# Sample attention first, its output weights split beside it; prompt attention and the sample's top-k moved into the output-projection stage

## The chip, the core and the metric

The kernel runs on one core of one Trainium2 chip. The metric is the device time of one execution in microseconds. On a core, TensorE (PE) multiplies, VectorE (DVE) and ScalarE (ACT) work elementwise, GpSimd (POOL) issues the indirect transfers and SyncE (SP) most of the others. Each engine takes its own instructions strictly in the order of the program and stops at a semaphore wait until it is met; whatever stands behind the wait on that engine waits too.

## What is computed

One encoder layer over two token sets that share all weights: a prompt of 512 tokens and a sample of 1024, width 1024. Cut to what matters:

```python
q, k, v, ca, cg = split(h @ w_in)                  # h: normed, modulated x
attn_out = neighbourhood_attention(q, k, v, rpb)   # 8 heads of 64, 8x16 window on a 64-wide grid
conv_out = conformer_conv(ca, cg, ...)
mix = concat([attn_out, conv_out], -1) @ w_out
x = x + gate1 * mix
h2 = rms_norm(x, norm2_g) * (1 + scale2) + shift2
aff = softmax(h2 @ w_router)                       # 16 experts
g, idx = top_k(aff.T, cap)                         # cap = 128 for the sample, 64 for the prompt
ye = swiglu(h2[idx], w_gate[e], w_up[e], w_down[e]) * g
x = x + gate2 * scatter_add(ye, idx)
```

The prompt and the sample are two sets: each expert takes the best 64 tokens of the prompt and the best 128 of the sample.

## The kernel before

Four functions follow each other, each with a block in which every engine has its own program; a block ends when all engines have ended theirs.

- `front`: per 128-token tile the norm of x and its transposes, the conditioning (`ada_w`, 12 loads of 2 MB), then the input projection as products of f32r high and low parts, with the convolution's taps on VectorE beside them. At its start VectorE first waits for all constants (`consts`, L691), and TensorE does so before the first transpose; the identity matrix is the first of them, issued on ScalarE's queue. The load of x tile t waits until tile t-3 has been normed.
- `attend`: 48 pairs of units in the order head pair, then block: 4 blocks of the prompt (256 keys) and 8 of the sample (384 keys) per head pair. A pair is: scores for two heads (TensorE), bias and maximum (L907, VectorE), exponential (L941, ScalarE), reciprocal and scaling (L914, L917), transposes (L862), their copy (L949), the product with v (L877), copy out (L926). The queues issue q and k of head pair 0, two heads' biases, 64 loads of v on SyncE and 32 on ScalarE, then the rest.
- `mix`: loads `w_out` (4 MB) and splits it into high and low parts (L1081, L1118), then 12 tiles in order, prompt first: split of the input (L1076 to L1113), 48 matmuls (L1041), gate and residual add (L1131, L1134), sum of squares (L1088), root, reciprocal, scaling (L1143), 8 transposes (L1051), modulation on ScalarE (L1096), the router's matmul (L1059), softmax, transpose (L1066), copy into `affT` (L1166). Tile t's matmuls, tile t-1's norm and tile t-2's softmax go side by side.
- `experts`: starts the weight loads; VectorE does 16 rounds of top-8 over `affT`, 48 rows x 1024 (rows 0 to 15 are the prompt's experts, 32 to 47 the sample's), each a MAX8 (L1506), FIND_INDEX8 (L1508) and MATCH_REPLACE8 (L1510). Then the lists are turned, POOL gathers the rows of expert 0 (L1358, L1360), and 16 experts follow. Each expert is bound by TensorE.

The text on record counts tiles of `mix` as steps 0 to 11, with two steps of run-out behind them.

Of the kernel before, what the change touches and what calls it, by code (L numbers as in the profile page):

```python
# [32 lines left out]
F32 = mybir.dt.float32  # L33
# [6 lines left out]
P = 128  # L40
# [41 lines left out]
def program(nc, A, outs):  # L82
# [29 lines left out]
    with g:  # L112
# [12 lines left out]
        affT = sb(g, "affT", [48, SAMPLE])  # L125
        o_ctx = ExitStack()
        with o_ctx:
            attn = sb(o_ctx, "attn", [P, 4, TOKENS])
            attend(nc, A, sem, sb, ps, qk_d, v_d, ident, attn)
            mix(nc, A, sem, sb, ps, rows_of, x_d, y_d, ada_d, conv_d, xhat_d, ident, eps_col, modv, a2, affT, attn)  # L130
        experts(nc, A, sem, sb, ps, y_d, ada_d, xhat_d, ident, modv, a2, affT)
# [31 lines left out]
def front(nc, A, sem, sb, ps, ada_d, rows_of, x_d, qk_d, conv_d, v_d,  # L163
# [49 lines left out]
    with ExitStack() as c:  # L213
# [49 lines left out]
        CONSTS = 16 * (5 + CG)  # L263
# [47 lines left out]
        with nc.Block() as block:  # L311
            @block.sync
            def _(sp):
# [18 lines left out]
                load_x(0)  # L332
                load_x(1)
# [67 lines left out]
            def _(pe):  # L401
# [40 lines left out]
                def side(job):  # L442
# [9 lines left out]
                    else:  # L452
                        pe.wait_ge(ada_row, MODS)
# [21 lines left out]
                pe.wait_ge(consts, CONSTS)  # L475
# [67 lines left out]
            def _(act):  # L543
                act.dma_start(ident[:, :], A["ident"]).then_inc(consts, 16)
# [6 lines left out]
                act.wait_ge(c_loaded, 32)  # L551
# [115 lines left out]
            def _(dve):  # L667
# [22 lines left out]

                dve.wait_ge(consts, CONSTS)  # L691
                dve.tensor_scalar(qkg[:, 0:1], qkg[:, 0:1], DH ** -0.5, None, ALU.mult).then_inc(qkg_ready, 1)
                for t in range(TILES):
# [6 lines left out]
                    if t == 5:  # L700
                        ada_rows(0)
# [76 lines left out]
def attend(nc, A, sem, sb, ps, qk_d, v_d, ident, attn):  # L778

    NB = len(BLOCKS)
    UNITS = HEADS * NB
    PAIRS = UNITS // 2
    PR = 6
    qk_loaded = [sem(f"qk_loaded{i}") for i in range(4)]
    v_loaded = [sem(f"v_loaded{i}") for i in range(len(V_ROWS))]
    bias_loaded = [sem(f"bias_loaded{i}") for i in range(4)]
    s_done, s_biased, p_ready, p_scaled = (
        sem("s_done"), sem("s_biased"), sem("p_ready"), sem("p_scaled"))  # L790
    pT_done, pT_out, o_done, r_ready, o_out = sem("pT_done"), sem("pT_out"), sem("o_done"), sem("r_ready"), sem("o_out")
# [858 lines left out]
```

## Time and profile before

| | us |
|---|---|
| median of 3 runs (range) | 3412.8 (3410.8 to 3413.2) |
| profiled execution: its own time | 3411.5 |
| its span | 3409.3 |
| mean granted TensorE clock | 0.965 |
| TensorE busy | 3169.9 (93%) |
| VectorE busy | 2298.9 (67%) |
| ScalarE busy | 1911.0 (56%) |

The page divides the span into 40 slices of 85 us. TensorE is at nine tenths or more in every slice behind the eleventh, in the sixth to eighth, which hold `attend`, at seven, and in the eleventh, the top-k, nearly idle. A stage's worth is therefore read from its own stretch and not from the busy shares of the span.

### The profile page before, as it was taken

What the parts mean: (1) busy time and instruction counts of PE and PEld (TensorE: products, weight loads), DVE (VectorE), ACT (ScalarE), POOL (GpSimd) and SP (SyncE); (2) the same over time, 40 slices, a digit from 0 to 9 for tenths busy, and PEclk for the clock granted to TensorE, in tenths of its full rate; (3) what the DMA queues carried; (4) which work ended last, traced back from release to release, by engine and by line L of the source; (5) the groups of instructions that cost most, each with busy time, mean ns of one, the idle gap of its engine ahead of it and who ended that gap; (6) DMA issues with size and microseconds to landing.
All of it is one profiled execution on the core that took longest, in us unless ns stands there. A gap on an engine that the chain in (4) does not pass through costs nothing.

```text
span 3409.3 us, 50511 instructions
## 1 busy us (share of the span) xinstructions
PE 3169.9 (93%) x18950; PEld 2832.9 (83%) x18950; DVE 2298.9 (67%) x3457; ACT 1911.0 (56%) x3096; POOL 150.8 (4%) x209
## 2 busy tenths in 40 slices
PE   5999877798099999999999999999999999999997
PEld 3777654587089999999999999999999999999997
DVE  4678815633757776767677776767677676767675
ACT  5143435655056666666666665666666666666654
POOL 0000000000000100101010010101010010101000
PEclk8999988999589999999999999999999999999999
DMA  8321137232345766657575765757576665757572
GB/s 308 130 62 53 47 100 248 104 131 93 146 178 218 264 231 241 241 201 275 193 288 218 251 237 226 254 206 277 194 273 226 241 250 221 263 187 278 210 253 87
DMA packets 136261, 690.67 MB, mean 203 GB/s; under 512 B 12032, under 2 KB 39824, under 8 KB 112528
## 3 DMA queue, kind: packets, MB, share of 16 engines
q1 hardware_dynamic: 125824, 659.68, 51.9%
q0 software_dynamic: 7168, 25.17, 3.2%
q10 hardware_dynamic: 3088, 3.10, 0.3%
q8 instruction: 152, 2.49, 0.3%
q14 instruction: 29, 0.24, 0.0%
HBM read 650.14 MB, written 37.77 MB: 202 GB/s over the span
## 4 chain that ended last, share of the span: by engine, by line
PE 72%; DVE 2%; DMA 0%; POOL 0%; ACT 0%; issue 0%; POOLq 0%; DVEq 0%
PE psG L1318 32%; PE psG L1320 15%; PE psY L1334 5%; PE psY L1337 5%; PE psY L1335 5%; PE psY L1336 5%; PE psY L1338 5%; DVE idxu L1508 1%; DVE affT L1510 1%; DVE vals L1506 1%; PE psG L1285 0%; PE psG L1286 0%; DMA xg_s<-xhat_d,inow 0%; ACT xst L1417 0%; DVE xe L1529 0%
## 5 line engine op out<-in xcount | busy, mean ns | idle before, releaser
L1318 PE MATMUL psG<-xe,w_gu_hi_part 128*128 128x384 f32 x5632 | 1630.8, 360 | 4.2 <-DVE xe L1529 4.2
L1320 PE MATMUL psG<-xe,w_gu_lo_part 128*128 128x192 f32 x5632 | 1411.3, 251 | 0.0
L1320 PEld LDWEIGHTS psG<-xe,w_gu_lo_part 128*128 128x128 f32 x5632 | 1076.9, 191 | 7.9
L1318 PEld LDWEIGHTS psG<-xe,w_gu_hi_part 128*128 128x128 f32 x5632 | 1058.9, 188 | 12.6 <-DVE xe L1529 4.6
L1519 DVE TENSOR_TENSOR w_gu_lo_part<-raw_gu,w_gu_hi_part 128x1024 fp32r<-128x1024 f32 x704 | 858.8, 1222 | 117.8 <-ACT w_gu_hi_part L1428 117.8
L1428 ACT ACTIVATE w_gu_hi_part<-raw_gu 128x1024 fp32r<-128x1024 f32 x704 | 741.2, 1055 | 13.1 <-DMA raw_gu<-in_w_gu 13.1
L1553 DVE TENSOR_TENSOR gu<-psG,low 128x384 f32<-128x384 f32 x352 | 195.7, 556 | 569.3 <-ACT low L1458 569.3
L1524 DVE TENSOR_TENSOR w_dn_lo_part<-raw_dn,w_dn_hi_part 128x1024 fp32r<-128x1024 f32 x352 | 431.0, 1224 | 0.5 <-ACT w_dn_hi_part L1439 0.5
L1458 ACT ACTIVATE low<-psG 128x384 f32<-128x384 f32 x352 | 172.0, 489 | 417.0 <-PE psG L1320 417.0
L1439 ACT ACTIVATE w_dn_hi_part<-raw_dn 128x1024 fp32r<-128x1024 f32 x352 | 367.7, 1045 | 0.8 <-PE psY L1338 0.8
L1417 ACT ACTIVATE xst<-psG,modv,a 128x128 f32<-128x128 f32 (+1 forms) x256 | 95.7, 425 | 392.2 <-PE psG L1320 325.4
L1334 PE MATMUL psY<-w_dn_hi_part,hs 128*128 128x512 f32 x704 | 282.6, 401 | 0.0
L1337 PE MATMUL psY<-w_dn_hi_part,hs 128*128 128x512 f32 x704 | 277.7, 394 | 0.0
L1335 PE MATMUL psY<-w_dn_lo_part,hs 128*128 128x512 f32 x704 | 276.5, 393 | 0.0
L1336 PE MATMUL psY<-w_dn_hi_part,hs 128*128 128x512 f32 x704 | 276.1, 392 | 0.0
L1338 PE MATMUL psY<-w_dn_lo_part,hs 128*128 128x512 f32 x704 | 274.2, 389 | 0.0
L663 DVE SCALAR_TENSOR_TENSOR shared<-shared,convp 128x1566 f32<-128x1566 f32 x120 | 221.9, 1849 | 3.5
L438 PE MATMUL psZ<-h_hi,w_hi 128*128 128x512 f32 x480 | 202.9, 423 | 8.0 <-DVE h_lo L716 8.0
L1473 ACT ACTIVATE hs<-hid 128x192 fp32r<-128x192 f32 x352 | 128.4, 365 | 144.5 <-DVE hid L1560 144.4
L439 PE MATMUL psZ<-h_lo,w_hi 128*128 128x512 f32 x480 | 189.5, 395 | 0.0
L440 PE MATMUL psZ<-h_hi,w_lo 128*128 128x512 f32 x480 | 189.4, 395 | 0.0
L1337 PEld LDWEIGHTS psY<-w_dn_hi_part,hs 128*128 128x128 f32 x704 | 132.0, 187 | 30.6
(161 smaller groups left out, 3185.3 us busy)
## 6 DMA issues: line engine op xcount, KB each, us to landing
raw_gu<-in_w_gu SPq DMA_DIRECT2D x176, 2048.0 KB, 7.9
raw_dn<-in_w_down SPq DMA_DIRECT2D x176, 1024.0 KB, 8.8
shared<-in_ada_w SPq DMA_DIRECT2D x12, 2048.0 KB, 9.7
bias<-in_bias SPq DMA_DIRECT2D x8, 1536.0 KB, 12.3
w_raw<-in_w_in SPq DMA_DIRECT2D x20, 512.0 KB, 5.6
qk_d<-shared SPq DMA_DIRECT2D x8, 768.0 KB, 3.8
qk<-qk_d SPq DMA_DIRECT2D x8, 768.0 KB, 11.5
out<-wo_raw SPq DMA_DIRECT2D x12, 512.0 KB, 2.6
```

The lines of the kernel that those rows point to most:

```text
L663: dve.scalar_tensor_tensor(out=dst, in0=src, scalar=convp[:, j, t:t + 1], in1=dst, op0=ALU.mult, op1=ALU.add).then_inc(conv_taps, 1)
L1318: pe.matmul(bank[:, 0:2 * CAP], wh, xe[:, k, :, :].rearrange("p a b -> p (a b)"), start=(k == 0), stop=False, skip_group_check=True)
L1320: mm = pe.matmul(bank[:, 0:CAP], wl, xe[:, k, 0, :], start=False, stop=(k == KD - 1), skip_group_check=True)
L1334: pe.matmul(psY[:, h, :], s_hi, wh, start=st, stop=False)
L1335: pe.matmul(psY[:, h, :], s_hi, wl, start=False, stop=False)
L1336: pe.matmul(psY[:, h, :], s_lo, wh, start=False, stop=en)
L1337: pe.matmul(psY[:, 2 + h, :], pp, wh, start=st, stop=False)
L1338: mm = pe.matmul(psY[:, 2 + h, :], pp, wl, start=False, stop=en)
L1428: act.activation(w_hi[:, i % 2, m], raw_gu[:, s, m, i % 2], ACT.Copy).then_inc(gu_hi, 1)
L1439: act.activation(d_hi[:, i % DS], raw_dn[:, s, i % 2], ACT.Copy).then_inc(dn_hi, 1)
L1519: dve.tensor_tensor(w_lo[:, i % 2, m], raw_gu[:, (i // 2) % RING_GU, m, i % 2], w_hi[:, i % 2, m].bitcast(F32), ALU.subtract).then_inc(gu_ ...
L1524: dve.tensor_tensor(d_lo[:, i % DS], raw_dn[:, (i // 2) % RING_DN, i % 2], d_hi[:, i % DS].bitcast(F32), ALU.subtract).then_inc(dn_lo, 1)
```

## The change

`attend` is replaced by `attend_sample`: the 32 sample pairs alone. q and k are loaded for the sample only, two head pairs deep; v comes column block by column block (blocks 0 and 1 on ScalarE's queue, 2 and 3 on SyncE's). The split of `w_out` stands in pairs 8 to 15, one row block per pair, with two raw buffers; each later raw load waits for a split two before it, and the loads for head pair 2 stand behind them on SyncE's queue.

`mix` takes the sample's 8 tiles first and the prompt's 4 last. The 16 prompt pairs stand in steps 1 to 4, two in a slot "a" and two in a slot "b" of each step, with their last transposes and products in step 5. The 48 matmuls of a tile are two halves of 24; slot a and the transposes stand between them, the router's matmul and slot b behind the second. The modulation is shared by ScalarE and VectorE. Raw x has 2 buffers, not 3.

The top-k is split: 16 rounds on the sample's 16 rows x 1024 and 8 on the prompt's 16 rows x 512. Of the sample's rounds 1, 2, 2, 2, 2 stand at the ends of steps 9 to 13; behind step 13 come the prompt's 8, then the sample's last 7. All of it stands now in `mix`, so the block of `experts` begins behind the top-k. In `front` the identity is loaded on SyncE's queue behind x tile 0, only it is waited for at the start, and the wait for all constants is moved to x tile 5.

```diff
+S_PAIRS = [(t, s, j) for t in range(HEADS // 2) for s in (1, 2) for j in range(COL_BLOCKS)]
+P_PAIRS = [(t, 0, j) for t in range(HEADS // 2) for j in range(COL_BLOCKS)]
...
-                pe.wait_ge(consts, CONSTS)
+                pe.wait_ge(c_loaded, 48)
...
+                def load_w(k):
+                    if k >= 2:
+                        sp.wait_ge(w_lo_ready, k - 1)
+                    sp.dma_start(w_raw[:, k % 2, :], A["w_out"][k * P:(k + 1) * P, :]).then_inc(w_loaded[k % 2], 16)
...
+                for k in range(KD):
+                    load_w(k)
+                for t in (2, 3):
+                    heads(t)
+                    biases(2 * t)
+                    biases(2 * t + 1)
...
+                    k = u - FIRST_SPLIT
+                    if 0 <= k < KD:
+                        dve.wait_ge(w_hi_ready, k + 1)
+                        dve.tensor_tensor(w_lo[:, k, :], w_raw[:, k % 2, :], w_hi[:, k, :].bitcast(F32),
+                                          ALU.subtract).then_inc(w_lo_ready, 1)
...
+                split(0)
+                for j in range(COL_BLOCKS):
+                    load_v(act, v, v_d, S["v"], j, 0, GROUPS)
+                for s in range(TILES + 2):
...
+                    if s < TILES:
+                        mix_half(s, 0)
+                    pair_work(s, "a")
...
+    ROUNDS_AT = {9: 1, 10: 2, 11: 2, 12: 2, 13: 2}
...
+                done = rounds[0]
+                for r in range(CAP_P // 8):
+                    top_round(slice(0, EXPERTS), slice(0, PROMPT), r, done + r)
+                for r in range(done, CAP_S // 8):
+                    top_round(slice(32, 48), slice(0, SAMPLE), r, CAP_P // 8 + r)
```

TensorE between the matmuls of two tiles in the middle of `mix`, before (`psXT` are the transposes, `psLog` the router):

```order
L1041 MATMUL psMix<-wo_hi,ml 128x512
L1051 MATMUL psXT<-ident,wo_raw 128x128 x8
L1059 MATMUL psLog<-wr,wo_raw 128x16 x8
L1066 MATMUL psLog<-ident,af 48x128
L1041 MATMUL psMix<-wo_hi,mh 128x512
```

The same engine behind the second half of a tile in step 3 of the changed kernel (`psSp` are the prompt's scores, `psPp` its transposes, `psXT<-pT_p` its products with v):

```order
L1174 MATMUL psMix<-wo_hi,ml 128x512
L1211 MATMUL psLog<-wr,h 128x16 x8
L1130 MATMUL psSp<-qk_p 128x256 x2
L1139 MATMUL psPp<-ident,pr_p 128x128 x4
L1152 MATMUL psXT<-pT_p,v_p 64x128 x8
L1130 MATMUL psSp<-qk_p 128x256 x2
L1139 MATMUL psPp<-ident,pr_p 128x128 x4
L1152 MATMUL psXT<-pT_p,v_p 64x128 x8
L1174 MATMUL psMix<-wo_hi,mh 128x512
```

Two prompt pairs have moved in front of the next tile's matmuls; two more, without the products, stand between its halves.

VectorE from the end of slot b of one step to the first bias of slot a of the next, in the changed kernel (`tg<-psMix` is the gate, of half a tile):

```order
L1321 RECIPROCAL rs_p<-sm_p 128x2
L1324 TENSOR_SCALAR pr_p<-pr_p,rs_p 128x256 x2
L1351 TENSOR_REDUCE lg<-psLog 128x1
L1353 TENSOR_SCALAR lg<-lg 128x1
L1294 TENSOR_TENSOR tg<-psMix,gate 128x512
L1359 TENSOR_TENSOR xt<-xt,tg 128x1024
L1363 RECIPROCAL lg<-lg 128x1
L1370 TENSOR_SCALAR af<-ex,lg 128x16
L1375 TENSOR_SCALAR st<-st 128x1
L1377 RECIPROCAL st<-st 128x1
L1379 TENSOR_SCALAR xh<-xt,st 128x1024
L1294 TENSOR_TENSOR tg<-psMix,gate 128x512
```

Behind the last row stands the bias of slot a. The scaling of the prompt pairs of slot b, the softmax of tile s-2, the norm of tile s-1 and the gate of half a tile thus follow one another on VectorE before slot a can begin.

VectorE at the end of step 11 in the changed kernel, from the gate to the next step:

```order
L1294 TENSOR_TENSOR tg<-psMix,gate 128x512
L1391 TENSOR_SCALAR h<-psXT,a,modv 128x128 x4
L1401 COPY affT<-psLog 16x128
L1332 MAX vals<-affT 16x8
L1334 MAX_INDEX idxu<-vals,affT 16x8
L1336 MATCH_REPLACE affT<-vals,affT 16x1024
L1332 MAX vals<-affT 16x8
L1334 MAX_INDEX idxu<-vals,affT 16x8
L1336 MATCH_REPLACE affT<-vals,affT 16x1024
L1351 TENSOR_REDUCE lg<-psLog 128x1
```

Two rounds of the sample's top-k stand ahead of the first instruction of the next step.

## Rows read from the trace of the kernel before

**Rows 1.** The page: the chain that ended last, by engine.
```profile
PE 72%; DVE 2%; DMA 0%; POOL 0%; ACT 0%; issue 0%; POOLq 0%; DVEq 0%
```

**Rows 2.** Windows (us, then per engine busy us and instructions, granted clock, DMA).
```profile
core 0: us, PE busy (x) PEld busy (x) DVE busy (x) ACT busy (x) POOL busy (x), PEclk, DMA share, GB/s
499.70:656.00 156.30, 118.00 (x960) 73.14 (x960) 92.96 (x384) 92.29 (x241) 0.00 (x0) 0.86 0.48 162
589.00:618.60 29.60, 27.62 (x242) 17.08 (x241) 23.16 (x97) 22.71 (x61) 0.00 (x0) 1.00 0.28 108
656.00:665.00 9.00, 0.01 (x1) 0.04 (x1) 2.54 (x4) 3.26 (x4) 1.06 (x2) 0.62 0.86 321
665.00:683.10 18.10, 15.44 (x48) 10.92 (x49) 9.75 (x9) 7.39 (x8) 0.00 (x0) 0.81 0.90 329
736.80:751.00 14.20, 13.81 (x76) 11.57 (x76) 5.63 (x12) 8.21 (x18) 0.00 (x0) 1.00 0.31 113
833.60:859.40 25.80, 12.24 (x68) 11.23 (x66) 6.88 (x22) 12.08 (x28) 0.09 (x1) 0.61 0.14 56
859.40:921.60 62.20, 0.34 (x1) 0.18 (x1) 60.58 (x81) 3.90 (x4) 0.86 (x1) 0.50 0.38 152
921.60:949.90 28.30, 5.44 (x18) 2.65 (x18) 6.89 (x9) 7.06 (x17) 9.56 (x16) 0.50 0.43 143
```

**Rows 3.** Start: timeline, and DMA rate in 40 slices of 0 to 110 us.
```profile
19.06 0.15 DVE L692 TENSOR_SCALAR qkg<-qkg 128x1 f32<-128x1 f32 x1 [19.06 <-DMA qkg<-in_qk_gain]
...
GB/s 30 238 305 309 328 337 154 25 359 395 408 414 411 407 401 414 408 350 313 298 396 411 416 371 362 398 116 0 27 343 407 183 82 408 276 0 186 417 252 399
```

**Rows 4.** Timeline at the start of attention.
```profile
499.71 15.58 ACTq L817 DMA_DIRECT2D v<-v_d  x32
...
517.06 0.42 DVE L907 CUSTOM_DVE_ANT_0 sc<-psSc,bias 128x256 f32<-128x256 f32 x1 [29.47 <-DMA bias<-in_bias]
...
529.81 1.12 PE L877 MATMUL psOh<-pT,v 128*64 128x128 f32 x8 [7.82 <-DMA v<-v_d]
```

**Rows 5.** Timeline, VectorE, the split of the output weights.
```profile
663.63 8.88 DVE L1118 TENSOR_TENSOR wo_lo<-wo_raw,wo_hi 128x1024 fp32r<-128x1024 f32 x7
```

**Rows 6.** Timeline and windows around a wait of TensorE in attention.
```profile
561.30 1.55 PE L877 MATMUL psOh<-pT,v 128*64 128x128 f32 x12 [4.69 <-ACT pT L949]
...
559.00:563.00 4.00, 1.70 (x13) 1.37 (x14) 3.38 (x16) 2.84 (x9) 0.00 (x0) 0.53 1.01 427
563.00:566.00 3.00, 3.00 (x16) 2.02 (x17) 0.49 (x3) 0.83 (x2) 0.00 (x0) 0.50 0.46 193
```

**Rows 7.** Groups by form, 12 pairs of attention, 589 to 618.6 us.
```profile
L907 DVE CUSTOM_DVE_ANT_0 sc<-psSc,bias 128x384 f32<-128x384 f32 x16 | 8.3, 555 | 3.4 <-PE psSc L855 3.3
...
L941 ACT ACTIVATE pr<-sc,nm 128x256 f32<-128x256 f32 x8 | 4.0, 501 | 1.6 <-DVE nm L907 1.6
...
L907 DVE CUSTOM_DVE_ANT_0 sc<-psSc,bias 128x256 f32<-128x256 f32 x8 | 3.1, 422 | 2.6 <-PE psSc L855 2.6
...
L917 DVE TENSOR_SCALAR pr<-pr,rs 128x256 f32<-128x256 f32 x8 | 2.5, 350 | 0.1
L949 ACT ACTIVATE pT<-psPT 128x512 f32<-128x512 f32 x4 | 2.3, 579 | 0.2 <-PE psPT L862 0.2
```

**Rows 8.** Timeline of one tile of the output projection.
```profile
758.84 1.06 ACT L1088 ACTIVATE wo_raw<-wo_raw 128x1024 f32<-128x1024 f32 x1 [3.75 <-DVE wo_raw L1134]
...
762.55 1.09 PE L1051 MATMUL psXT<-ident,wo_raw 128*128 128x128 f32 x8 [0.39 <-DVE wo_raw L1143]
...
763.48 1.86 PE L1059 MATMUL psLog<-wr,wo_raw 128*128 128x16 f32 x16
```

**Rows 9.** Timeline behind the last tile's matmuls.
```profile
846.08 1.97 PE L1051 MATMUL psXT<-ident,wo_raw 128*128 128x128 f32 x8 [9.83 <-DVE wo_raw L1143]
```

**Rows 10.** Chain of waits behind the top-k.
```profile
928.93 10.64 DMA xg_s<-xhat_d,inow
```

**Rows 11.** DMA issues, 960 to 3390 us: size and median us to landing.
```profile
xg_s<-xhat_d,inow POOLq DMA_INDIRECT x14, 5.7
```

More of the change, by code:

```diff
@@ L857, in turn @@
[L857 to L872 removed]
+                    if u % 8 == 0:
+                        pe.wait_ge(S["qk"][t], 32)
@@ L880, in pv @@
-                    mm.then_inc(o_done, 1)
-                for u in range(PAIRS + 3):
-                    if u < PAIRS:
-                        scores(2 * u)
-                        scores(2 * u + 1)
+                                           v[:, (first + m) * COL_BLOCKS + j, (2 * t + w) * DH:(2 * t + w + 1) * DH], pT[:, u % 2, m, w, :],
+                                           start=(m == 0), stop=(m == 2))
+                    mm.then_inc(S["o_done"], 1)
+                for u in range(NS + 3):
+                    if u < NS:
+                        scores(u)
@@ new lines, in mix @@
+    SLOTS = {}
+    for n in range(NP // 2 + 1):
+        step, which = 1 + n // 2, "ab"[n % 2]
+        SLOTS[step, which] = dict(new=[g for g in (2 * n, 2 * n + 1) if g < NP],
+                                  old=[g for g in (2 * n - 2, 2 * n - 1) if g >= 0], pv=[])
+    LAST = 1 + NP // 4
+    SLOTS[LAST, "b"] = dict(new=[], old=[], pv=[])
+    for step in range(2, LAST + 1):
+        SLOTS[step, "b"]["pv"] = list(range(4 * (step - 2), 4 * (step - 1)))
+    PROMPT_AT = SAMPLE // P
+    NOTHING = dict(new=[], old=[], pv=[])
@@ new lines, in pv_before @@
+    def pv_before(s):
+        return sum(len(w["pv"]) for (step, _), w in SLOTS.items() if step < s)
+    ROUNDS_AT = {9: 1, 10: 2, 11: 2, 12: 2, 13: 2}
+    with ExitStack() as c:
+        qk = sb(c, "qk_p", [P, 2, 2, PROMPT])
+        v = sb(c, "v_p", [P, GROUPS * COL_BLOCKS, WA])
+        bias = sb(c, "bias_p", [P, 4, 3, 256])
+        attn_p = sb(c, "attn_p", [P, 4, PROMPT])
+        sc = sb(c, "sc_p", [P, 2, 256])
+        pr = sb(c, "pr_p", [P, PR, 256])
+        pT = sb(c, "pT_p", [P, 4, 2, 2, P])
+        nm = sb(c, "nm_p", [P, 4])
+        sm = sb(c, "sm_p", [P, 4])
+        rs = sb(c, "rs_p", [P, 4])
+        conv = sb(c, "conv3", [P, CR, 4, P])
+        gate1 = sb(c, "gate1", [P, 2, D])
@@ new lines, in pair_work, with mix_half @@
+                def pair_work(s, which):
+                    todo = SLOTS.get((s, which), NOTHING)
+                    for x in range(2):
+                        for g in todo["new"][x:x + 1]:
+                            scores(g)
+                        for g in todo["old"][x:x + 1]:
+                            turn_p(g)
+                        for g in todo["pv"][2 * x:2 * x + 2]:
+                            pv(g)
+                def mix_half(q, n):
+                    if n == 0:
+                        pe.wait_ge(m_lo, q + 1)
+                    if q >= 1:
+                        pe.wait_ge(gated, 2 * (q - 1) + n + 1)
+                    for k in range(KD):
+                        for i, (m, w) in enumerate(((mh, w_hi), (mh, w_lo), (ml, w_hi))):
+                            mm = pe.matmul(psM[:, n, :], m[:, q % 2, k, :], w[:, k, n * 512:(n + 1) * 512],
+                                           start=(k == 0 and i == 0), stop=(k == KD - 1 and i == 2))
+                    mm.then_inc(mixed, 1)
```

718 lines of the change are left out of this document (425 added, 293 removed).

## The prediction, on record before the changed kernel was run

> **What bounds the kernel now.** I read the page first: the chain that ended last is 72% TensorE, nearly all of it in the experts, which the change leaves alone [rows 1]. So the question is how long it takes until the first expert starts, at 949.9 us. The windows cut this into stages [rows 2]: attention 156.3 us (its last third runs at 29.6 us for 12 pairs, TensorE 27.6 busy: bound there by TensorE), 9.0 until the first output matmul, 18.1 for the first tile with the weight split, then tiles of 14.2 us with TensorE 13.8 busy, 25.8 from the last tile's matmuls to the top-k, 62.2 of top-k, in which VectorE alone works, and 28.3 to the first expert matmul. The timeline says what waits where: at the start VectorE for a constant that landed at 19.06, with a hole in the DMA rate in the two slices of 2.75 us that follow [rows 3]; at the start of attention for the biases until 517.06 and for v until 529.81 [rows 4]. The sum is made on the profiled run (3411.5 us, its span 2.2 less), which lies 1.3 below the median.
>
> **Front: -4.5 us.** Norms may start at about 10 us instead of 19. But the transfers bind behind it: rates stay near 400 GB/s until about 55 us, apart from the slices at 154 and 25 GB/s [rows 3]. Filling them gives (1 - 154/400 + 1 - 25/400) x 2.75 = 4.3 us, not 9; everything behind moves with it. Bounds 2 and 7.
>
> **Attention: -38 us.** Without prompt pairs 32 remain. A sample pair takes about 2.55 us (29.6 for 8 sample and 4 prompt pairs, the latter shorter by a tenth). At the start, q, k and two biases are 3.4 MB and not 4.6, v is 4.2 and not 6.3; the v loads of a queue are issued one in 0.49 us (32 in 15.58 [rows 4]). I put the first product at 519 and the second, held by block 1 of v, at 525.5 (529.8 before). The last of 32 is then at 525.5 + 30 x 2.55 = 602. To this the split adds 8 VectorE instructions of 1.27 us (8.88 for 7 [rows 5]), where VectorE has 23.2 of 29.6 us busy [rows 2] and so 0.5 us a pair to spare: 8 us with the wait for ScalarE's half. And a new wait: the loads for head pair 2 (q and k 1 MB, biases 2.4 MB) stand on SyncE's queue behind the last raw weights, which wait for the split of pair 13; 3.9 MB at some 427 GB/s [rows 6] and 2 us of latency are 11 us, pair 16 comes 7 us after: 4 to 6 us of stall. Sum 602 + 8 + 5 + 2.5 = 617.5 against 656. Bounds -44 (no stall, split half hidden) and -32.
>
> **To the first matmul: -1.** One small tile of the convolution is waited for and not 1 MB.
>
> **The output stage: +52.** Before, 665.0 to 833.6, 168.6 us. After, by steps, counting from the end of a tile's matmuls T:
>
> - Tile 0 costs 11.15 for its matmuls and up to 3 at half clock. ScalarE then issues 32 loads of v (15.6 us as above) before it splits tile 1, so that TensorE's tile 1 starts 14.7 us behind tile 0's start either way. Step 1 ends at 28.5.
> - Steps 2 to 4. TensorE has 13.8 + 4 pairs x 1.75 = 20.8 us of work. But the order on VectorE makes a chain. Slot b: after the router's 1.86, scores 0.75, bias 0.45, two exponentials 1.4, copy 0.6, transposes and products 1.6, copy out, scaling 2 x 0.85 (forms in [rows 7]): its last scaling at T + 8.6. Then softmax maximum and negation 0.4, half gate 0.65, add 1.25, and 3.7 from square to transposes (758.84 to 762.55 [rows 8]): T + 14.6. Then half a gate 0.65, and slot a's bias 0.45, exponentials and copy until TensorE's last transposes at 17.8; tile transposes 1.0 and the second half 5.6: T + 24.4. Three such steps 73.2, step 5 (last transposes) 21.3, step 6 (last products) 17.2: tile 6 at 140.
> - Steps 7 to 10: the same chain without pairs. Router 1.86, maximum 0.4, gate 0.65, add 1.25, 3.74, plus 1.1 and 5.6 = 14.65 a step; before it was 14.2 with the router beside the norm and not ahead of it. 58.6 us.
> - Rounds. One is 62.2/16 = 3.89 us. In a step VectorE is free from 12.6 (10.3 in step 11) to 16.5: one round in step 9 costs nothing, two in step 10 cost 3.9, two in step 11 cost 1.6, paid in the run-out. Tile 11 ends at 217.
> - Clock. In attention, a wait of 4.7 us that ended at 561.3 left TensorE at a granted 0.53 and 0.50 of full clock until 566 [rows 6]: 1.7 to 3.4 us of work lost. In steps 2 to 4 TensorE idles 2.5 and 2 us in the same slot, in step 10 about 4. I take half of the cases: +4.
>
> Sum 217 + 4 - 168.6 = +52. Bounds +38 (TensorE-bound steps of 22, no dips) and +64.
>
> The Trainium skill, "TensorE: Matmul & The Clock Gate", section "HAM oscillation — how this bites in real kernels", says that a kernel whose matmul groups are separated by repeated waits falls back to the lower clock at each of them. By it, all five long-wait steps would pay 1.7 to 3.4 us and the stage would be +57 rather than +52. The trace agrees as far as one wait of 4.7 us can show it [rows 6]; for pairs of waits of 2 us no row shows it.
>
> **Run-out and top-k: -12.** Before, 25.8 + 62.2 = 88.0 from T. After: rounds of step 11 until T + 3.5, then 0.4 + 0.65 + 1.25 + 3.7 = 9.5, transposes 1.8 at half clock (row at 846.08 [rows 9]), modulation and copy: 12.7; two rounds 20.5; softmax of the last tile 2, two rounds: 30.3. Then 8 prompt rounds: three instructions over 512 columns and not 1024. The bias instruction takes 555 ns for 384 columns and 422 for 256 [rows 7], 0.53 us for 512 columns; at that slope a round is 3.89 - 1.6 = 2.29, 18.3 for eight. Seven sample rounds 27.2: T + 75.8. The same 16 sample rounds are run, and 8 prompt rounds, which before rode on the same instructions, are new. No row shows these instructions over 512 columns: at half a round, 1.95, the term is -15; at a whole one, 3.89, it is +0.6.
>
> **Expert start: +1.** Before, 9.4 MB of expert weights (62.2 us at 152 GB/s [rows 2]) came under the top-k, now they begin with the gather. But the gather took 10.64 us [rows 10], with 3 MB of weights beside it, against 5.7 in the expert loop [rows 11]; it already shared the engines. At the rate of the top-k's window's transfers in full flow, some 400 GB/s, the first 3 MB are there 10 us into the block, the gather ends at 18, and the splits run in between. Bounds 0 and 9 (the gather behind all 9.4 MB).
>
> **Sum.** -4.5 - 38 - 1 + 52 - 12 + 1 = -2.5: 3409 on the profiled run, 3410 on the median.
>
> **Rivals.**
>
> - *The steps overlap better* (clearly faster). If slot chains hide behind matmuls, steps 2 to 4 take TensorE's 20.8 and a little, 22, and the clock holds: +41 in place of +52, and attention without its stall -42. Total about 3395. For it: TensorE's own work in the stage rises by only 28 us. Against: VectorE's order above.
> - *The output stage becomes a chain with a falling clock* (slower). One mechanism: TensorE waits in both slots of steps 1 to 6 and after the double rounds, and each time runs on at half clock. From three dips on at 3.4 us each, with the queue order above, the sum passes +7. With seven it is +20: 3432. For it: the dip of [rows 6], and tiles of 14.2 us that had 0.4 to spare. Against: before, the dips came after single waits of over 4.7 us.
> - *The gather lands late* (slower): +9 for the weights that came under the top-k, 3418. Against: it already ran at a shared rate.
>
> **How the numbers follow.** A measurement of this kernel tells a change of over 0.2% (6.8 us) from none. My sum lies near zero, with terms of 40 to 50 us on both sides, each good to some 6. No difference: 0.36. The overlap rival and errors to its side: faster 0.36. The clock chain 0.17, the late gather and other stalls 0.11: slower 0.28. The likeliest single time is 3410; its own range, from the bounds taken two at a time, is 3398 to 3422; with the rivals 3393 to 3430.
>
> **What would show it.** The first DMA hole gone and the input projection starting at 60.5, not 65. The last attention copy near 617, a wait for the biases of heads 4 and 5 at its pair 16. First matmul of tile 1 waiting for ScalarE's split. Steps 2 to 4 at 24.4 us, steps 7 to 9 at 14.65, step 11 at 18.5. Top-k ended 76 us behind the last output matmul, the first expert matmul 29 us later. I would be wrong if steps 2 to 4 take below 22 or above 27, if the granted clock falls in them, or if the prompt's round is far from 2.3.

## The result, and the profile after

| | before | after |
|---|---|---|
| median of 20 runs each, us | 3412.5 | 3418.0 |
| lowest and highest, us | 3409.4, 3415.1 | 3413.9, 3419.5 |
| span of the profiled execution, us | 3409.3 | 3416.3 |
| ratio, 95% interval | | 1.0015, 1.0009 to 1.0021 |

The changed kernel is 5.6 us slower, where 2.5 faster was forecast. The time lies within the predicted range; the sign does not. With 20 runs on each side the interval is narrower than the 0.2% that the prediction took as the limit of a measurement.

The page of the changed kernel, as [rows 1]: span, busy time, the clock in 40 slices, and the chain by engine.

```profile
span 3416.3 us, 50585 instructions
...
PE 3182.5 (93%) x18950; PEld 2842.4 (83%) x18950; DVE 2333.4 (68%) x3557; ACT 1894.2 (55%) x3050; POOL 146.6 (4%) x210
...
PEclk8999989999589999999999999999999999999999
...
PE 72%; DMA 0%; DVE 0%; ACT 0%; POOL 0%; issue 0%; POOLq 0%; DVEq 0%
```

The share of TensorE on the chain did not move; only the eleventh slice is at a low clock, as before. VectorE's 2% is gone from the chain because the page follows it back to the start of the block of `experts` only, and the top-k now stands ahead of that block. The stages show what happened. Windows of the changed kernel, as [rows 2]: attention, up to the first output matmul, tile 0, tile 3, tile 6, tile 11, run-out, the rest of the top-k, and up to the first expert matmul.

```profile
495.15:622.16 127.01, 88.36 (x704) 54.95 (x704) 75.22 (x264) 73.55 (x169) 0.00 (x0) 0.87 0.54 175
...
622.16:628.31 6.15, 0.00 (x1) 0.01 (x1) 1.58 (x3) 1.15 (x2) 0.46 (x3) 0.67 0.69 191
628.31:644.99 16.68, 14.29 (x48) 11.03 (x48) 2.04 (x4) 1.15 (x2) 0.00 (x0) 0.81 1.08 279
689.36:714.53 25.17, 22.97 (x139) 18.08 (x137) 14.01 (x49) 13.12 (x35) 0.00 (x0) 0.93 0.36 122
759.09:773.79 14.70, 14.23 (x75) 11.69 (x74) 7.09 (x18) 6.83 (x13) 0.00 (x0) 1.00 0.37 126
832.82:853.07 20.25, 15.47 (x62) 12.44 (x61) 16.02 (x30) 5.79 (x11) 0.00 (x0) 0.83 0.13 52
853.07:873.60 20.53, 7.57 (x43) 6.91 (x41) 15.05 (x31) 6.15 (x13) 0.00 (x0) 0.58 0.13 51
873.60:927.76 54.16, 0.28 (x2) 0.03 (x1) 51.70 (x87) 0.00 (x0) 0.04 (x1) 0.50 0.00 0
927.76:956.96 29.20, 5.74 (x19) 2.78 (x19) 7.78 (x9) 10.97 (x21) 6.42 (x17) 0.50 0.96 373
```

Set against the stages of before, in us (attention is cut at the start of the last copy, the top-k at the start of the next block; the last round itself ends at 927.44):

| stage | before | after | change | predicted |
|---|---|---|---|---|
| until attention starts | 499.7 | 495.15 | -4.6 | -4.5 |
| attention | 155.9 | 127.0 | -28.9 | -38 |
| to the first output matmul | 9.4 | 6.15 | -3.2 | -1 |
| output matmuls, first to last | 168.6 | 224.8 | +56.2 | +52 |
| to the end of the top-k | 87.9 | 74.7 | -13.2 | -12 |
| to the first expert matmul | 28.4 | 29.2 | +0.8 | +1 |
| all experts | 2459.5 | 2459.4 | -0.1 | 0 |
| sum | | | +7.0 | -2.5 |

Four terms came within 2.2 us. Attention missed by 9.1 and the output stage by 4.2, both upwards. Both are read in the timeline. The start of attention, on VectorE, TensorE and its weight load (PEld):

```profile
513.12 0.56 DVE L922 CUSTOM_DVE_ANT_0 sc<-psSc,bias 128x384 f32<-128x384 f32 x1 [29.96 <-DMA bias<-in_bias]
...
519.38 1.55 PE L895 MATMUL psOh<-pT,v 128*64 128x128 f32 x12
...
523.11 0.63 PEld L895 LDWEIGHTS psOh<-pT,v 128*64 128x64 f32 x12 [0.67 <-ACT pT L970]
```

The first biases are there 18.0 us behind the start of the stage, where before it was 17.4 ([rows 4], from 499.7), and neither the first nor the second product waits for v. In attention, a pair that carries a part of the weight split (ScalarE, VectorE):

```profile
551.95 1.04 ACT L964 ACTIVATE wo_hi<-wo_raw 128x1024 fp32r<-128x1024 f32 x1
551.96 0.28 DVE L940 COPY attn_s<-psOh 128x128 f32<-128x128 f32 x1
...
553.02 1.23 DVE L944 TENSOR_TENSOR wo_lo<-wo_raw,wo_hi 128x1024 fp32r<-128x1024 f32 x1 [0.78 <-ACT wo_hi L964]
```

VectorE is done with the pair's own work 0.28 us behind 551.96 and waits 0.78 us for the high half, which ScalarE begins only behind the pair's two exponentials. This repeats in each of the eight pairs: they take 4.0 us, a plain one 2.6. The end of this stretch, on SyncE's queue and on VectorE:

```profile
558.29 0.33 SPq L843 DMA_DIRECT2D wo_raw<-in_w_out  x1
558.67 0.91 SPq L833 DMA_DIRECT2D qk<-qk_d  x2
...
571.82 0.56 DVE L922 CUSTOM_DVE_ANT_0 sc<-psSc,bias 128x384 f32<-128x384 f32 x1 [5.51 <-DMA bias<-in_bias]
```

The loads of q and k for head pair 2 are issued right behind the last raw weights, and its biases are there 13 us later, at 571.8. In the output stage, the first tiles on ScalarE and VectorE:

```profile
628.02 14.40 ACTq L800 DMA_DIRECT2D v_p<-v_d  x29
642.46 0.63 ACT L1223 ACTIVATE mh<-attn_s 128x512 fp32r<-128x512 f32 x1 [15.54 <-issue]
...
643.64 0.69 DVE L1289 TENSOR_TENSOR ml<-attn_s,mh 128x512 fp32r<-128x512 f32 x1 [5.84 <-ACT mh L1224]
```

ScalarE's issue of v is over at 642.4, and only then does it split tile 1. Tile 11, where the transposes wait for the norm that stands behind the two top-k rounds of step 10:

```profile
843.46 1.97 PE L1191 MATMUL psXT<-ident,xh 128*128 128x128 f32 x8 [4.78 <-DVE xh L1379]
```

### The profile page after: what moved, and what is told of

Its sections match the earlier page's. It is cut to its first block, busy times and chain, and to the rows that moved or that the text cites. A ratio compares the mean times of both kernels' runs of the same rounds, so it can differ in the third digit from the quotient of the medians.

```text
span 3416.3 us, 50585 instructions
## 1 busy us (share of the span) xinstructions
PE 3182.5 (93%) x18950; PEld 2842.4 (83%) x18950; DVE 2333.4 (68%) x3557; ACT 1894.2 (55%) x3050; POOL 146.6 (4%) x210
## 4 chain that ended last, share of the span: by engine, by line
PE 72%; DMA 0%; DVE 0%; ACT 0%; POOL 0%; issue 0%; POOLq 0%; DVEq 0%
PE psG L1559 32%; PE psG L1561 15%; PE psY L1575 5%; PE psY L1578 5%; PE psY L1576 5%; PE psY L1577 5%; PE psY L1579 5%; PE psG L1526 0%; DMA xg_s<-xhat_d,inow 0%; PE psG L1527 0%; ACT xst L1658 0%; DVE xe L1761 0%; POOL out L1614 0%; ACT xe L1684 0%; POOL out L1616 0%
## 6 DMA issues: line engine op xcount, KB each, us to landing
shared<-in_ada_w SPq DMA_DIRECT2D x12, 2048.0 KB, 10.7
```

## The experiments

The code lines given are cut to what is changed.

**The early start alone.** The kernel before with the edit of `front`.

```diff
-                pe.wait_ge(consts, CONSTS)
+                pe.wait_ge(c_loaded, 48)
```

> The kernel before, with the edit of front alone (identity on SyncE's queue, later wait for the constants). Theory, the hole in the DMA rate is filled and everything behind moves with it: 4 us faster (3408.4 where before is 3412.5), the input projection from 60.9 us, not 65.0, and attention from 495.2, not 499.7. Rival, later loads meet others and give part of it back: under 2 us.

Measured: 3408.9, ratio 0.9987 (0.9978 to 0.9996), 3.6 us below the kernel before; attention starts at 494.8 in place of 499.7. The term of -4.5 is shown. In the profiles 4.2 of the 4.9 us reach the end; one gap in attention, behind the eighth copy, is 8.4 us where it was 7.1.

**Another order of loads in attention.** The changed kernel; head pair 2 stands between the raw weights.

```diff
-                for k in range(KD):
-                    load_w(k)
-                for t in (2, 3):
-                    heads(t)
+                load_w(0)
+                load_w(1)
+                heads(2)
+                load_w(2)
+                load_w(3)
+                biases(4)
+                load_w(4)
+                biases(5)
```

> The changed kernel, with the loads of q, k and biases for head pair 2 put between the raw weights on SyncE's queue instead of behind them. Theory, the stall at pairs 16 to 18 of attention (copies 9.6 and 5.3 us apart where 2.6 is usual) is the queue order and was sized too low: attention 8 to 10 us shorter, the whole 3409. Rival, the raw weights now come late and the split waits instead, or the loads are bound by bandwidth: under 3 us gained.

Measured: 3410.2, ratio 0.9991 (0.9982 to 1.0), 7.9 below the changed kernel. The attention window:

```profile
494.38:612.96 118.58, 86.13 (x704) 53.34 (x704) 75.24 (x264) 73.42 (x169) 0.00 (x0) 0.90 0.57 187
```

118.6 us, 8.4 less. The gap of 9.6 us between two copies is gone, the eight split pairs still take 4.0 us each. The stall was worth 8.4 us, where the prediction had 4 to 6.

**VectorE's half one pair later.** The changed kernel.

```diff
-                    k = u - FIRST_SPLIT
+                    k = u - FIRST_SPLIT - 1
                     if 0 <= k < KD:
                         dve.wait_ge(w_hi_ready, k + 1)
```

> The changed kernel, with VectorE's half of the weight split one pair later, so that it does not wait for ScalarE's half of the same pair. Theory, the split costs 1.4 us a pair and not 1.0 because VectorE waits 0.78 us in each for ScalarE: pairs of 3.3 us and not 4.0, 5 to 6 us in all unless the stall of head pair 2, whose loads are released by the split, takes it. Rival, the pair is bound by ScalarE and TensorE with the split in it: no gain, pairs stay at 4.0.

Measured: 3417.9, ratio 1.0016; no gain, attention takes 127.4 us for 127.0. The pairs became uneven (2.4 to 5.3 us) and one gap grew to 13.9: the two raw buffers are now released a pair later, so the next weights and, behind them on the same queue, head pair 2 came later. It could not tell the wait from the work; the run with three raw buffers, below, does.

**No scaling of the prompt's probabilities.** The changed kernel; leaves out the reciprocals and the scaling of the 16 prompt pairs in `mix`, so the prompt's softmax is not normalised; TensorE's transposes then wait for ScalarE's exponential and no longer for VectorE's scaling.

```diff
-                        dve.reciprocal(rs[:, 2 * u % 4:2 * u % 4 + 2], sm[:, 2 * u % 4:2 * u % 4 + 2]).then_inc(S["r_ready"], 1)
-                        for i in (2 * u, 2 * u + 1):
-                            dve.tensor_scalar(pr[:, i % PR, :], pr[:, i % PR, :], rs[:, i % 4:i % 4 + 1], None,
```

> The changed kernel without the reciprocals and the scaling of the prompt's probabilities (left out of the computation), two reciprocals and four scalings of a slot, 1.7 us of VectorE. Theory, steps 2 to 4 are a chain through VectorE's order in which slot b's scaling comes ahead of the norm: each of steps 2 to 5 is 1.5 to 2 us shorter, 7 us in all. Rival, these steps are bound by TensorE or by ScalarE's copies: steps of 25 to 26 us as before, under 2 us in all.

Measured: 3409.9, ratio 0.9991; the output stage 218.6. One full step, the fourth tile:

```profile
689.20:711.46 22.26, 21.50 (x139) 16.64 (x137) 11.17 (x37) 12.90 (x35) 0.00 (x0) 1.00 0.41 140
```

With 2.8 us of VectorE's work taken out, steps of 23.2, 25.2 and 26.1 become steps of 22.2, 22.3 and 22.3 with TensorE 21.5 busy. Not all of that is VectorE's. The two longer steps of the changed kernel hold a stretch at half clock, and this run has none there. The same step at full clock stands in the kernel with no top-k round among the tiles, which has the same code here:

```profile
689.99:713.71 23.72, 21.51 (x140) 16.65 (x138) 14.02 (x49) 12.90 (x35) 0.00 (x0) 1.00 0.39 130
```

Against it the scaling is worth 1.0 to 1.5 us a step, of the 1.7 to 2.2 that TensorE stands still, where 1.5 to 2 were expected. So at full clock steps 2 to 4 wait for VectorE's order, as the rows of that order ahead of the prediction had it, but by some 2 us and not more.

**The prompt pairs left out, of both kernels.** Their work is not computed, and the prompt's attention columns are zero. In the changed kernel:

```diff
+    SLOTS.clear()
...
+                pool.memset(attn_p[:, :, :], 0.0).then_inc(aff_zero, 1)
```

> The changed kernel with the prompt's attention pairs left out (their loads, scores, softmax, transposes and value products; the prompt's attention columns are zeroed instead), so the work of 16 pairs is not computed. Theory (a pair costs more among the output tiles than in the attention loop, since six tiles wait for VectorE there): the stretch from first to last output matmul falls from 224.8 us to about 12 x 14.7 plus the double rounds, 182, that is by 40 to 47, and the time to about 3375. Rival (the pairs cost in the output stage what they cost in the attention loop, 2.33 each): the stretch falls by 37, to 188.

and in the kernel before:

```diff
-BLOCKS = [(s, j) for s in range(3) for j in range(COL_BLOCKS)]
+BLOCKS = [(s, j) for s in (1, 2) for j in range(COL_BLOCKS)]
```

> The kernel before with the prompt's 16 attention pairs left out in the same way (prompt columns zeroed). Both theories: the attention stage falls by 16 x 2.33 = 37 us, to about 3375. The difference between this fall and that of the changed kernel is the price of moving the pairs: 3 to 10 us by the theory, nothing by the rival.

Measured: 3372.9, 45.1 below the changed kernel, and 3375.2, 37.6 below the kernel before. (The changed kernel was not timed again beside these two; the kernel before was, 0.3 us from its other median.) The windows, the output matmuls of the first and attention of the second:

```profile
627.96:806.37 178.41, 169.58 (x837) 138.82 (x837) 92.71 (x207) 73.71 (x139) 0.00 (x0) 0.97 0.35 119
```

```profile
499.99:623.93 123.94, 90.01 (x704) 55.83 (x704) 66.16 (x256) 66.21 (x161) 1.80 (x1) 0.82 0.54 187
```

So the 16 pairs cost 46.4 us among the output tiles (224.8 less 178.4), 2.9 each, and 37.6 of time before, 2.35 each. Of the 37.6 the window of attention holds 32.0 and the output matmuls 3.0. By the two falls in time, the move itself costs 7.5 us. Without pairs the two kernels stand 2.3 apart, the changed one ahead.

**No top-k round among the tiles.** The changed kernel.

```diff
-    ROUNDS_AT = {9: 1, 10: 2, 11: 2, 12: 2, 13: 2}
+    ROUNDS_AT = {9: 0, 10: 0, 11: 0, 12: 0, 13: 0}
```

> The changed kernel with no top-k round among the last output tiles: all of the prompt's rounds run behind the last tile, beside the sample's. Theory (the overlap of the rounds is worth their time on VectorE, less what the double rounds made the last tiles wait): 9 prompt rounds more at the end; a prompt round takes 2.3 to 3.9 us there, so 21 to 35 us more behind the last matmul, 5 less ahead of it, together +16 to +30, about 3434 to 3448. Rival (the rounds only stand beside the sample's anyway): within 5 us of the changed kernel, 3413 to 3423.

Measured: 3431.1, ratio 1.0057, 13.1 above the changed kernel, less than the theory's bound. (The nine rounds moved are the sample's; the text on record calls them the prompt's. Three of them stood ahead of the last matmul.) Windows of the output matmuls and of what follows until the top-k ends:

```profile
626.55:842.00 215.45, 199.98 (x1093) 159.34 (x1093) 105.12 (x313) 99.18 (x221) 0.00 (x0) 0.98 0.41 133
842.00:939.74 97.74, 7.84 (x42) 6.94 (x42) 83.96 (x140) 6.15 (x13) 0.04 (x1) 0.51 0.03 11
```

23.0 us more behind the last matmul (97.7 for 74.7), 9.3 less ahead of it. Of these, tile 11 gives 7.2 (13.0 for 20.25) and tiles 3 and 4 give 3.9 for a reason that has nothing to do with the rounds (the clock, below); step 10 gives 0.6, and the first two steps are 2.4 longer.

**The pairs and the split put back.** The kernel before with the early start, the sample first and the overlapped rounds, its 48 pairs in attention and the weight split at the start of `mix`. Against the changed kernel, for the split:

```diff
+                for k in range(KD):
+                    act.wait_ge(w_loaded[k], 16)
+                    act.activation(w_hi[:, k, :], w_raw[:, k, :], ACT.Copy).then_inc(w_hi_ready, 1)
```

> The kernel before with three parts of the change: the early start of the weights, the sample's tiles first in the output stage, and the prompt's top-k rounds beside its last tiles; the 48 attention pairs and the split of the output weights stay where they were. Theory (moving the prompt's pairs and splitting the weights beside the sample's gave nothing, the other parts are the gain): 3412.5 less 4.2 (start) less 13 (behind the last matmul) plus about 5 (double rounds) plus 1 gives about 3401. Rival (sample first without the pairs in between runs the last tiles at a lower clock or the split costs its 8 x 1.1 again): 3410 or more.

Measured: 3407.4, ratio 0.9984 (0.9975 to 0.9993). Faster than both kernels, by 5.1 and 10.7, but 6 short of the theory:

```profile
657.82:840.20 182.38, 169.64 (x837) 139.05 (x837) 101.82 (x215) 82.15 (x148) 0.00 (x0) 0.96 0.39 136
840.20:915.17 74.97, 7.85 (x43) 6.94 (x42) 67.03 (x118) 6.15 (x13) 0.04 (x1) 0.52 0.04 14
```

The 13 us behind the last matmul are there (75.0 for 87.9), but the output matmuls take 182.4 for 168.6. Of these 13.8, tile 11 is 8.9 (20.1 for 11.2), tiles 1 and 2 are 3.3, step 10 is 0.9, each other step of the new code 0.1 to 0.3 (14.45 for 14.2), and tile 0 is 0.8 shorter. So the sample's tiles first, the split top-k and its overlap come together to about nothing (13.8 less 12.9); what is gained stands ahead of them, where the first output matmul comes 7.2 us earlier: 4.0 from the start, 1.1 in attention and 2.1 behind it.

**One round in step 10.** The changed kernel.

```diff
-    ROUNDS_AT = {9: 1, 10: 2, 11: 2, 12: 2, 13: 2}
+    ROUNDS_AT = {9: 1, 10: 1, 11: 2, 12: 2, 13: 2}
```

> The changed kernel with one top-k round in step 10 in place of two; the round moves behind the last step. Theory (the second round of step 10 makes VectorE late for tile 10's norm, so TensorE waits 4.8 us in step 11 and runs on at half clock): tile 11's matmuls take about 13 to 14 us in place of 20.3, 3.9 us are given back behind them, and the time falls by 3 to 4 us, to about 3414.5. Rival (the wait belongs to the doubled rounds of step 11 or to the step itself): it rises by 0 to 4 us.

Measured: 3416.7, ratio 1.0011 (1.0002 to 1.002), 1.4 below, which the intervals (1.0009 to 1.0021 for the changed kernel) can't tell from nothing. The wait and the dip of tile 11 went (13.6 us for 20.3), but the last tile's transposes now waited longer (7.98 us for 6.08):

```profile
856.99 1.97 PE L1191 MATMUL psXT<-ident,xh 128*128 128x128 f32 x8 [7.98 <-DVE xh L1379]
```

and the top-k ended at 927.79, against 927.76. From tile 11 on, VectorE is the chain: what TensorE waits for there costs nothing by itself.

**Two pairs in a step.** The changed kernel; scores in slot a, transposes and products in slot b, over seven steps.

```diff
+    ORDER = [(0, "b"), (1, "a"), (1, "b"), (2, "a"), (3, "a"), (4, "a"), (5, "a"), (6, "a")]
+    OLD = [(1, "a"), (1, "b"), (2, "a"), (2, "b"), (3, "b"), (4, "b"), (5, "b"), (6, "b")]
+    PV_AT = [1, 2, 2, 3, 4, 5, 6, 6]
```

> The changed kernel with the same 16 prompt pairs spread over seven output tiles, two in a step (four in step 1) and not four in each of four steps: scores, bias and exponential in slot a, transposes and products in slot b. Theory (the pairs are dear because two slots of softmax follow each other on VectorE in one step; with one slot the step is TensorE's 17.3 us or a little more): steps 2 to 6 take 17.5 to 19 us, step 1 about 22, and the output stage falls by 10 to 15 us, the time to 3403 to 3408. Rival (a pair costs the same wherever it stands, 2.9 us): 3418.

Measured: 3418.0, as the rival said. Steps 3 to 5 are 18.4 to 18.6 us, as expected, but the first three are 22.9, 22.6 and 22.8, and step 6 is 19.9. Step 0:

```profile
642.32 0.63 ACT L1224 ACTIVATE mh<-attn_s 128x512 fp32r<-128x512 f32 x1 [16.07 <-issue]
...
648.57 0.42 DVE L1311 CUSTOM_DVE_ANT_0 sc_p<-psSp,bias_p 128x256 f32<-128x256 f32 x1 [3.77 <-issue]
649.06 1.56 PE L1131 MATMUL psSp<-qk_p 64*128 64x256 f32 x4 [7.45 <-DVE nm_p L1311]
```

The scores stood ready at 641.6 and ScalarE issued until 642.3, but the biases landed at 648.45, behind v, q and k on the same DMA engines, and VectorE's first bias add follows at 648.57. This run left open whether a pair costs the same wherever it stands, or the early steps wait for something else.

**The three mends together.** The order of loads, one round in step 10, and two pairs in a step.

> The changed kernel with three mends together: the other order of loads in attention, one round in step 10, and the prompt pairs spread two to a step. Theory (the three costs are apart and add): 3418.0 less 7.9 less 3.5 less 12 is about 3394.6, 18 us below the kernel before. Rival (they hide one another, or the pairs' loads come late when the steps are short): above 3403.

Measured: 3409.9, ratio 0.9993 (0.9984 to 1.0002): the same as the order of loads alone, as the two runs above let one expect.

**Order of loads, a later low half, a third raw buffer.** The changed kernel.

```diff
-        w_raw = sb(c, "wo_raw", [P, 2, D])
+        w_raw = sb(c, "wo_raw", [P, 3, D])
...
-                    k = u - FIRST_SPLIT
+                    k = u - FIRST_SPLIT - 1
```

> The changed kernel with the other order of loads (head pair 2 ahead of the last raw weights), VectorE's low half of the weights one pair behind ScalarE's high half, and a third raw buffer so that the loads are not held by it. Theory (of the 1.4 us that the split adds to a pair, 0.78 is VectorE's wait for ScalarE): split pairs of 3.3 to 3.6 us and not 4.0, 3 to 6 us less than with the order alone, 3404 to 3407. Rival (the split adds its own 1.3 us of VectorE whatever it waits for): 3410.

Measured: 3403.6, ratio 0.998 (0.9971 to 0.9989); again, on another occasion, 3405.9, ratio 0.9979 (0.997 to 0.9988). A split pair on VectorE now:

```profile
551.39 0.28 DVE L947 COPY attn_s<-psOh 128x128 f32<-128x128 f32 x1
551.59 1.22 DVE L951 TENSOR_TENSOR wo_lo<-wo_raw,wo_hi 128x1024 fp32r<-128x1024 f32 x1
...
554.93 0.56 DVE L929 CUSTOM_DVE_ANT_0 sc<-psSc,bias 128x384 f32<-128x384 f32 x1 [2.12 <-PE psSc L881]
```

and TensorE's scores and ScalarE's half just ahead of the last row:

```profile
553.25 1.65 PE L881 MATMUL psSc<-qk 64*128 64x384 f32 x4
...
553.81 1.06 ACT L971 ACTIVATE wo_hi<-wo_raw 128x1024 fp32r<-128x1024 f32 x1 [1.27 <-DMA wo_raw<-in_w_out]
```

No wait is left ahead of the low half; undisturbed split pairs take 3.1 us for 4.0. But the window of attention is 116.25 for 118.58, 2.3 less and not the 7 of 8 x 0.9: two pairs take 5.4 and 5.0 us, where a raw block lands 1.27 us late beside the biases and TensorE runs its scores in 1.65 us, at half clock, in place of 0.92. The single times of this kernel spread over 9.4 and 7.5 us, those of most others over 4 to 6. Both profiles are from its upper half, so what the faster executions do better was not seen.

**Early loads in the output stage.** The kernel above, its base on this occasion (the first text), and two with tile 0's and tile 1's data and two biases first, and v issued by SyncE behind them: one with the pairs as in the change, one with two pairs in a step.

```diff
+                load_gate(1)
+                load_x(0)
+                heads(0)
+                bias_of(0)
+                bias_of(1)
+                load_conv(1)
+                load_x(1)
...
+                    load_v(sp, v, v_d, S["v"], j, 0, GROUPS)
...
-                    load_v(act, v, v_d, S["v"], j, 0, GROUPS)
```

> The mended attention again, on the same chip as the two that follow, as their base. Both theories: 3403 to 3408, as before.

> The mended attention, and in the output stage another order of loads: tile 0's, then head pair 0 and two biases, tile 1's, then the rest; the prompt's v is issued by SyncE behind them and no longer by ScalarE ahead of its split of tile 1. The pairs stand as in the changed kernel. Theory (the first two steps wait for ScalarE's issue and the loads): steps 0 and 1 fall from 18.1 + 22.3 to about 14 + 21, and the stage by 4 to 6 us. Rival (steps 1 to 4 are VectorE's order and the v issue is hidden by TensorE's tile 0): within 1.5 us of the mended attention alone.

> As e13_early, with the pairs spread two to a step from step 0 on. In e10_spread step 0 took 22.9 us, of which 7.5 were a wait of the first scores' successors for a bias that landed late. Theory (that wait was the loads, and goes): steps 0 and 1 about 17 + 22, steps 2 to 6 18.5, the stage 8 to 11 us shorter than that of the mended attention alone, 3393 to 3399. Rival (sixteen pairs cost 43 us however they stand): as e13_early, above 3400.

Measured: 3397.5, ratio 0.9957 (0.9944 to 0.9971), and 3397.1, ratio 0.9954 (0.9941 to 0.9968); 8.4 and 8.8 below their base. ScalarE's split of tile 1, and the output matmuls, of the first of the two:

```profile
620.63 0.63 ACT L1237 ACTIVATE mh<-attn_s 128x512 fp32r<-128x512 f32 x1 [7.56 <-DMA conv<-conv_d]
```

```profile
614.45:830.63 216.18, 202.35 (x1093) 161.49 (x1093) 121.48 (x336) 99.64 (x221) 0.00 (x0) 0.96 0.40 132
```

The split stands 6.2 us behind the first matmul and no longer 14.2; it now waits for tile 1's own data. Steps 0 and 1 take 13.0 and 20.0 for 18.2 and 22.2, the stage 216.2 for 225.8. The pairs now cost 216.2 - 178.4 = 37.8 us of this stage, 2.36 each, about the 37.6 that they cost before the move. In times, 45.1 less 8.4 is 36.7. Both sums book all of the gain on the pairs: the kernel without pairs was not run with this order of loads. Two in a step gives 217.9, no less: steps 3 to 5 are 18.4 to 18.6, but steps 1 and 2 take 23.8 and 24.1, where 22 and 18.5 were expected. What these two wait for was not followed up. So both theories were partly right: the excess was the wait of the first steps, and given that, the spread gives nothing.

## Why the prediction was wrong

**The step that failed is "Attention: -38 us".** It measured -28.9. By its own sum, counted on the clock of before (4.6 added to the changed kernel's times): the second copy came at 532.1, where 525.5 and the 2.5 of its sum give 528, so 4.0 late; the split took 10.8 us and not 8; the stall 9.6 and not 5; the rest ran 2.2 faster than 30 x 2.55. Together 9.2. The split and the stall were named, with sizes that were too low; of the start the mechanism was wrong as well:

- *The start.* The second product, "held by block 1 of v", did not wait for v (the 529.8 set beside it is the first product of before, [rows 4]). The fewer bytes did not bring the first biases earlier (18.0 us behind the start of the stage, for 17.4). On the clock of before, the first product came at 524.0 and not at 519, the second at 527.7, behind ScalarE's copy of its transposes (0.67 us, row at 523.11). From there to its copy it was 4.4 us and not 2.5. No run changed these loads, so what would bring the biases earlier stays open.
- *The split.* It took "0.5 us a pair to spare" for VectorE and added "the wait for ScalarE's half" to a total without a term of its own. That wait was 0.78 us in each of eight pairs. With the low half a pair later it is gone (3.1 us a pair), which is shown; how much of the whole time it is worth, 2 to 7 us, stays open.
- *The stall.* The wait itself is 5.5 us on VectorE (571.82, above), within "4 to 6". What was left out is what it leaves behind: TensorE stood for 6.1 us and ran the next pairs at half clock, as in [rows 6], so that they came 5.3 and 2.9 us apart. The window of that stretch:

```profile
573.10:579.90 6.80, 5.43 (x30) 3.69 (x32) 3.60 (x14) 3.63 (x10) 0.00 (x0) 0.50 0.86 333
```

  The prediction priced the clock in the output stage and not here. The other order of loads gave 8.4 in the window of attention and 7.9 in the time, so wait and aftermath together are shown.

**The output stage** was off in its first tile, and in its chain the agreement is partly luck. Ends of the tiles' matmuls, from the first matmul:

| tile | 1 | 4 | 5 | 6 | 10 | 11 |
|---|---|---|---|---|---|---|
| predicted | 28.5 | 101.7 | 123.0 | 140 | 198.6 | 217 + 4 |
| measured | 33.0 | 106.3 | 127.0 | 143.9 | 203.0 | 224.8 |

Steps 2 to 4 were 73.3 us in place of 73.2, but 3.9 of these are the clock's, which the prediction had booked apart: at full clock, in the kernel with no round among the tiles, the same three are 69.4, so "T + 24.4" was 1.3 us a step too long. Its sign of being wrong, "if the granted clock falls in them", came true. Steps 5 and 6 were 20.7 and 16.9 in place of 21.3 and 17.2. "Step 1 ends at 28.5" was 4.5 short: it saw that ScalarE issues 32 loads of v ahead of its split of tile 1, but let TensorE begin 14.7 us behind tile 0's start (16.7) and left out what slot a of step 1 adds between the halves (3.1). The first half of tile 1 also began with 3.4 us at half clock, and took 7.3 us where one at full clock takes 5.9. In the run with early loads tile 1 ends at 27.7. Tiles 7 to 10 were 59.0 for 58.6. The last tile took 21.8 for 18.4 and the 4 of the clock: the doubled rounds held up the norm as foreseen. That this wait cost the whole next to nothing is shown by the run with one round.

**The clock.** Taken as +4 for the whole stage; tiles 3 and 4 alone show 3.9, and tiles 1 and 11 hold a dip as well. These windows of the changed kernel hold a wait and what follows, between the halves of tile 4, and the dip of tile 11:

```profile
721.60:723.30 1.70, 0.07 (x2) 0.04 (x1) 1.70 (x5) 1.04 (x2) 0.00 (x0) 0.99 0.13 53
723.30:730.10 6.80, 6.76 (x23) 5.51 (x24) 4.92 (x18) 5.69 (x16) 0.00 (x0) 0.50 0.59 181
...
842.70:849.60 6.90, 6.14 (x19) 5.22 (x20) 5.36 (x10) 2.79 (x5) 0.00 (x0) 0.51 0.19 76
```

A wait of 1.63 us was followed by 6.8 us at 0.50, that is at 1.2 GHz in place of 2.4. The kernel with no rounds among the tiles has the same wait, 1.63 us, at 720.8, and keeps the full clock:

```profile
718.00:724.00 6.00, 3.85 (x19) 2.25 (x17) 3.24 (x12) 5.30 (x11) 0.00 (x0) 1.00 0.50 178
724.00:730.00 6.00, 5.95 (x33) 5.08 (x34) 4.43 (x15) 3.90 (x11) 0.00 (x0) 1.00 0.39 129
```

There tiles 3 and 4 take 23.7 and 23.7 us, in the changed kernel 25.2 and 26.1: 3.9 us for the two dips.

The prediction held against a falling clock that "before, the dips came after single waits of over 4.7 us". The trace of before shows another, in its first output tile, behind a wait of 1.72 us:

```profile
675.25 0.79 PE L1041 MATMUL psMix<-wo_hi,mh 128*128 128x512 f32 x1 [1.72 <-DVE wo_lo L1118]
...
675.30:678.60 3.30, 3.30 (x8) 2.62 (x9) 1.29 (x2) 0.00 (x0) 0.00 (x0) 0.50 0.72 219
```

The Trainium skill, "TensorE: Matmul & The Clock Gate", section "HAM oscillation — how this bites in real kernels", tells of a kernel in which each wait was longer than the matmuls between two of them, and each brought the clock down. The prediction applied it to waits far shorter than the work between them. For these the traces agree in part: of the three steps with four pairs two dipped in the changed kernel and none in the other, while tile 11's wait of 4.8 us, still shorter than the work ahead of it, did bring a dip. The +57 stands near the measured +56.2 for other reasons, the late tile 1 above all; it is also the low end of its own prices, since five steps at 1.7 us make +57 and at 3.4 us +65.

**Front, run-out, expert start** held. The prompt's round was forecast from the slope of another instruction at 2.29 us. The groups by form behind the last tile, of the changed kernel:

```profile
L1332 DVE MAX8 vals<-affT 16x8 f32<-16x512 f32 x8 | 5.5, 682 | 0.3
L1334 DVE FIND_INDEX8 idxu<-vals,affT 16x8 uint32<-16x512 f32 x8 | 5.4, 673 | 0.0
L1336 DVE MATCH_REPLACE8 affT<-vals,affT 16x512 f32<-16x512 f32 x8 | 5.3, 664 | 0.0
```

With two value loads of 0.08 that is 2.18 us of work, and the whole term was -13.2 for -12. The late gather of the rivals did not come: the chain of waits has 14.61 us for the gathered rows (10.64 in [rows 10]), yet the stretch to the first expert matmul grew by 0.8 alone.

**The sum.** The two large terms, -38 and +52, missed by 24% and 8%, both upwards, 13.3 us; the small ones gave 3.8 back. A sum of -2.5 between two such terms could not carry a sign.

**The rivals.** "The steps overlap better" failed at steps of 23.2 to 26.1, though at full clock, 23.2 to 23.7, they stood about midway between its 22 and the 24.4; "a chain with a falling clock" named two things that were there, the chain and the dips, but there were four dips (tiles 1, 3, 4 and 11) and not seven, at some 1.5 us for one of 3.4 us and 2.4 for one of 6.8; its sums also put the dips on top of the +4 that the forecast already held, without which three make +3.7 and seven +17; "the gather lands late" did not decide anything.

## What to carry to other kernels

Moving work from one stage to another gives only the difference of its two prices. Here 16 pairs cost 2.35 us each in the kernel before and 2.36 among the output tiles once the waits there were mended, so the move could give nothing, and every new wait (32 loads issued by a computing engine, a queue entry behind a blocked one, a half that waits for another engine's half) was a loss. When such a move shows no gain, look first at the first steps of the new stage and at what stands behind the last throttled load on each queue: putting those in order, with a third raw buffer and the low half one pair later, gave 20.5 us here, from 3418.0 to 3397.5, and made the version that beats the kernel before by 0.43%.

Leave the moved work out of both kernels, and compare the two falls: that prices the move without an argument over overlap.

## What was unexpected of the hardware

Equal waits of TensorE (1.63 us, at the same place of the program in two tiles running) were followed by a granted clock of 0.50 in one kernel and of 1.00 in another, though the code of these tiles is the same in both. The run with one round has that code too. Its three waits, 1.16 us in tile 2, 1.64 in tile 3 and 1.63 in tile 4, were followed by dips in tiles 2 and 3 and by none in tile 4. The dip of its tile 2, which had none in the changed kernel:

```profile
678.60:681.90 3.30, 3.30 (x14) 2.85 (x13) 2.36 (x7) 3.13 (x9) 0.00 (x0) 0.50 0.54 179
```

Its tiles 2 to 4 take 24.8, 25.0 and 23.7 us, against 23.2, 23.7 and 23.7 without a dip. A dip is therefore no property of a wait of this length alone, and the same code can have it in one tile or another; whether it also moves between executions of one kernel was not seen, since each trace is of a single execution. The two of the changed kernel cost 3.9 us, as much as many an edit. A wait of 4.8 us in tile 11 was followed by 0.51 here, as the one of 4.7 in [rows 6].
